# Gating mix with the high and low parts of its weights side by side in one product of 256 columns, and the last B gate placed between its groups

## The reference, cut to what matters

```python
def spatial_gating(u, v, ln_g, ln_b, w_s, b_s):
    v = layer_norm(v, ln_g, ln_b)
    vb = v.reshape(b, nb, SGU_BLOCK, SGU_GROUPS, SGU_GROUP_DIM)      # 4 blocks of 128 tokens, 4 groups of 128
    w = jnp.where(mask[None], w_s, jnp.zeros_like(w_s))              # 4 matrices, 128 x 128
    mixed = jnp.einsum('gts,bnsgc->bntgc', w, vb) + b_s.T[None, None, :, :, None]
    return u * mixed.reshape(b, s, SGU_WIDTH)
...
y_b = (multiscale_pool(b_x, pool_w[i], pool_scale[i]) * jax.nn.silu(b_z)) @ w_b_out[i]
```

## Time and profile before

| what | value |
|---|---|
| median of 3 runs | 1369.49 us (1369.45 to 1371.21) |
| profiled execution | 1370.01 us, span of its trace 1368.2 us |
| PE busy | 1357.1 us, 99% of the span |
| DVE, ACT, POOL busy | 709.3, 561.5, 555.1 us |
| mean granted TensorE clock | 0.999 of full speed |

### The profile page before, as it was taken

How to read it: one execution, slowest core, us unless ns; L and a number is a source line. 1 busy time by engine, 2 the same in 40 slices (tenths; PEclk the granted TensorE clock), 3 DMA queues, 4 the chain that set the end, 5 groups by cost and what they waited for, 6 DMA issues and landing times.

```text
span 1368.2 us, 15972 instructions
## 1 busy us (share of the span) xinstructions
PE 1357.1 (99%) x6426; PEld 1141.0 (83%) x6426; DVE 709.3 (52%) x1063; ACT 561.5 (41%) x871; POOL 555.1 (41%) x233
## 2 busy tenths in 40 slices
PE   9999999999999999999999999999999999999998
PEld 8778888888888888888888888888888888888887
DVE  7986454155553333265768864451555532242743
ACT  6554463355552222224444554542555422222242
POOL 2334242534334444444353442424433444444443
PEclk9999999999999999999999999999999999999999
DMA  7222222322222323322242222222322222323232
GB/s 213 87 68 85 75 93 65 93 80 90 77 78 98 102 92 94 122 93 93 92 116 93 72 90 70 84 62 93 92 78 77 92 93 93 106 94 108 98 100 95
DMA packets 67834, 126.56 MB, mean 92 GB/s; under 512 B 8480, under 2 KB 37424, under 8 KB 67760
## 3 DMA queue, kind: packets, MB, share of 16 engines
q1 hardware_dynamic: 66528, 124.98, 28.8%
q10 hardware_dynamic: 1232, 0.55, 0.1%
HBM read 123.41 MB, written 2.10 MB: 92 GB/s over the span
## 4 chain that ended last, share of the span: by engine, by line
PE 89%; DVE 7%; ACT 2%; DMA 1%; SPq 1%; issue 0%; ACTq 0%; DVEq 0%
PE ps L484 29%; PE ps L486 29%; PE ps L485 29%; DVE n_t L1430 1%; DVE trail_a L1466 1%; DVE h_lo L1305 1%; PE ps L733 1%; PE ps L668 1%; PE ps L769 1%; PE ps L655 1%; ACT w_hi L941 0%; DVE trail_b L1466 0%; DMA pos_i<-pos_in 0%; SPq L396 0%; DVE small L1447 0%
## 5 line engine op out<-in xcount | busy, mean ns | idle before, releaser
L459 POOL TENSOR_TENSOR w_lo<-w_raw,w_hi 128x1024 fp32r<-128x1024 f32 x222 | 546.4, 2465 | 787.8 <-ACT w_hi L941 787.8
L484 PE MATMUL ps<-h_hi,w_hi 128*128 128x512 f32 (+1 forms) x1160 | 453.1, 391 | 1.4 <-DVE h_lo L1305 1.3
L486 PE MATMUL ps<-h_hi,w_lo 128*128 128x512 f32 (+1 forms) x1160 | 450.5, 388 | 0.0
L485 PE MATMUL ps<-h_lo,w_hi 128*128 128x512 f32 (+1 forms) x1160 | 450.3, 388 | 0.0
L941 ACT ACTIVATE w_hi<-w_raw 128x1024 fp32r<-128x1024 f32 x227 | 238.5, 1054 | 169.7 <-PE ps L486 164.9
L484 PEld LDWEIGHTS ps<-h_hi,w_hi 128*128 128x128 f32 x1160 | 218.0, 188 | 47.7 <-DVE h_lo L1305 4.1
L486 PEld LDWEIGHTS ps<-h_hi,w_lo 128*128 128x128 f32 x1160 | 217.9, 188 | 44.7
L485 PEld LDWEIGHTS ps<-h_lo,w_hi 128*128 128x128 f32 x1160 | 218.1, 188 | 43.3
L1750 DVE SCALAR_TENSOR_TENSOR m_part<-th,ps 128x512 f32<-128x512 f32 x48 | 33.0, 688 | 236.9 <-PE ps L486 236.8
L1169 ACT ACTIVATE th<-ps 128x512 f32<-128x512 f32 x48 | 28.7, 597 | 182.0 <-PE ps L486 182.0
L484 PE MATMUL ps<-act_hi,w_hi 128*128 128x512 f32 x192 | 75.3, 392 | 0.0
(11 more groups left out here) (324 smaller groups left out, 1923.0 us busy)
## 6 DMA issues: line engine op xcount, KB each, us to landing
w_raw<-w_in SPq DMA_DIRECT2D x180, 512.0 KB, 3.5
w_raw<-w_in SPq DMA_DIRECT2D x92, 128.0 KB, 2.4
w_raw<-w_in SPq DMA_DIRECT2D x36, 256.0 KB, 2.9
x<-x_in SPq DMA_DIRECT2D x8, 256.0 KB, 3.7
w_raw<-w_in SPq DMA_DIRECT2D x32, 64.0 KB, 2.1
out_x<-x SPq DMA_DIRECT2D x7, 256.0 KB, 4.0
p_raw<-p_in SPq DMA_DIRECT2D x2, 512.0 KB, 4.4
w_raw<-w_in ACTq DMA_DIRECT2D x4, 128.0 KB, 3.0
```

Of the source, the lines that this page charges most:

```text
L459: pool.tensor_tensor(w_lo_t[s][:], w_raw_t[s][:], w_hi_t[s][:].bitcast(F32), ALU.subtract).then_inc(w_lo_made, 1)
L484: pe.matmul(o, a_hi, b_hi, start=first, stop=False, skip_group_check=skip)
L485: pe.matmul(o, a_hi, b_lo, start=False, stop=False, skip_group_check=skip)
L486: return pe.matmul(o, a_lo, b_hi, start=False, stop=last, skip_group_check=skip)
```

## The change

The low part of the mix weights is no longer kept in `w_lo_t`, but in the unused second half of the chunk's `w_hi_t` tile. One matmul with the stationary `vn_hi` then streams 256 columns, the high and the low weights of the group (`w_both[:, g::G, :]`), into 256 columns of PSUM, and a second one adds `vn_lo` by the high weights to the first 128 of them. A layer has 32 mix matmuls in place of 48. The two halves are added when DVE takes the mix out: two ops a group in place of one, with a wait between them. A group now needs two banks: groups 0 and 2 are in banks 0 and 1, groups 1 and 3 in banks 2 and 3.

So the order changes too: PE computes groups 0 and 1, then `bz3`, then groups 2 and 3, which wait for `mix_taken` of groups 0 and 1. `bz3` goes to bank 4 and no longer waits for `off_made`; `gb` and `yb` of the first pair take banks 5 and 4 (before 4 and 5), those of the second 6 and 7 as before. DVE makes `rope_tables` before quarter 2 of branch B, and quarter 3 between the groups. ACT does the tanh of `bz3` before the high part of `gb0`.

```diff
-BZ_BANKS, K_BANK = (7, 4, 6, 5), (6, 4)
+BZ_BANKS, K_BANK = (7, 4, 6, 4), (6, 4)
+GATE_BANK, TURN_BANK = (5, 6), (4, 7)
...
-                    pool.tensor_tensor(w_lo_t[s][:, 0:n, :], w_raw_t[s][:, 0:n, :], w_hi_t[s][:, 0:n, :].bitcast(F32),
+                    pool.tensor_tensor(w_hi_t[s][:, G:2 * G, :], w_raw_t[s][:, 0:G, :], w_hi_t[s][:, 0:G, :].bitcast(F32),
                                        ALU.subtract).then_inc(mix_lo_made, 1)
...
+                def mix(g):
+                    last = None
+                    for t in range(TB):
+                        o, v = (g % 2 * 4 + t) * 2 * P, slice(g * P, (g + 1) * P)
+                        pe.matmul(ps[:, o:o + 2 * P], vn_hi[:, t, v], w_both[:, g::G, :], start=t % 2 == 0, stop=False,
+                                  skip_group_check=True)
+                        last = pe.matmul(ps[:, o:o + P], vn_lo[:, t, v], w_both[:, g, :], start=False, stop=True,
+                                         skip_group_check=True)
+                    last.then_inc(mix_ready if g < G - 1 else done(l, "mix"), 1)
+
+                pe.wait_ge(pooled, after(l * G + 3))
+                pe.wait_ge(v_made, after(l * TB + 3))
+                pe.matmul(bank(5), ones_r[:], w_both[:, 0:G, :], start=True, stop=False)
+                pe.matmul(bank(5), ones_r[:], w_both[:, G:2 * G, :], start=False, stop=True).then_inc(wsum_ready, 1)
                 pe.wait_ge(ln_made, after(l * TB + TB - 1))
-                for g in range(G):
-                    pe.wait_ge(pooled, after(l * G + g))
-                    for t in range(TB):
-                        last = mm3(ps[:, g * 512 + t * P:g * 512 + (t + 1) * P], vn_hi[:, t, g * P:(g + 1) * P],
-                                   vn_lo[:, t, g * P:(g + 1) * P], w_hi[:, g, :], w_lo[:, g, :])
-                    last.then_inc(mix_ready if g < G - 1 else done(l, "mix"), 1)
-                pe.wait_ge(off_made, after(l))
-                project(l, "bz3", 5)
+                mix(0)
+                mix(1)
+                pe.wait_ge(act_b_made, after(l * G + 1))
+                project(l, "bz3", 4)
+                pe.wait_ge(mix_taken, after(l * G))
+                mix(2)
+                pe.wait_ge(mix_taken, after(l * G + 1))
+                mix(3)
...
                     if p == 0:
-                        pe.wait_ge(mix_taken, after(l * G + t))
+                        if t % 2 == 0:
+                            pe.wait_ge(mix_taken, after(l * G + 2 + t // 2))
...
-                act.wait_ge(*end_of(l, "mix"))
+                bz(3, 4)
                 weights_up_to(l, "gb0")
-                bz(3, 5)
                 b_high(3)
...
+                    o = g % 2 * 8 * P
+                    both = ps[:, o:o + 8 * P].rearrange("p (t u s) -> p t u s", t=TB, u=2)
+                    to = mix_t[:, g, :].rearrange("p (t s) -> p t s", t=TB)
+                    settle(dve.scalar_tensor_tensor(to, both[:, :, 1, :], sm("ln_col", g),
+                                                    over(mix_off[:, g, :], [P, TB, P], 1), ALU.mult, ALU.add))
+                    dve.scalar_tensor_tensor(to, both[:, :, 0, :], sm("ln_col", g), to, ALU.mult, ALU.add).then_inc(
+                        mix_taken, 1)
...
+                mix_taken_out(0)
+                mix_taken_out(1)
                 gate_z(3)
                 gate_p(3)
+                mix_taken_out(2)
+                mix_taken_out(3)
                 b_low(3)
```

More of the change, by code:

```diff
@@ L467, in _ @@
                     kept = keep[:].unsqueeze(1).broadcast_to([P, G, P // 2])
-                    part_hi, part_lo = w_hi_t[s][:, 0:G, 0:P // 2], w_lo_t[s][:, 0:G, 0:P // 2]
+                    part_hi, part_lo = w_hi_t[s][:, 0:G, 0:P // 2], w_hi_t[s][:, G:2 * G, 0:P // 2]
                     pool.tensor_tensor(part_hi, part_hi.bitcast(F32), kept, ALU.mult).then_inc(mix_hi_kept, 1)
@@ L609, in front @@
                 project(l, "bz2", 6)
-                w_hi, w_lo = chunk(l, "mix")
-                pe.matmul(bank(5), ones_r[:], w_hi[:, 0:G, :], start=True, stop=False)
-                pe.matmul(bank(5), ones_r[:], w_lo[:, 0:G, :], start=False, stop=True).then_inc(wsum_ready, 1)
-                pe.wait_ge(ln_made, after(l * TB + TB - 1))
-                for g in range(G):
-                    pe.wait_ge(pooled, after(l * G + g))
-                    for t in range(TB):
-                        last = mm3(ps[:, g * 512 + t * P:g * 512 + (t + 1) * P], vn_hi[:, t, g * P:(g + 1) * P],
-                                   vn_lo[:, t, g * P:(g + 1) * P], w_hi[:, g, :], w_lo[:, g, :])
-                    last.then_inc(mix_ready if g < G - 1 else done(l, "mix"), 1)
-                pe.wait_ge(off_made, after(l))
-                project(l, "bz3", 5)
+                w_both, _ = chunk(l, "mix")
+                def mix(g):
[11 more added lines that the diff above has]
+                pe.matmul(bank(5), ones_r[:], w_both[:, G:2 * G, :], start=False, stop=True).then_inc(wsum_ready, 1)
+                pe.wait_ge(ln_made, after(l * TB + TB - 1))
+                mix(0)
[6 more added lines that the diff above has]
+                mix(3)
             def gate_b(l, d, b, before, n):
@@ L687, in pair_c @@
                 k_at = slice(2 * PAIR * QK, 2 * PAIR * QK + PAIR * P)
-                kb, fill = K_BANK[p], 10 - K_BANK[p]
+                kb, gate, turn = K_BANK[p], GATE_BANK[p], TURN_BANK[p]
                 if p == 0:
@@ L710, in pair_c @@
                 if p == 0:
-                    gate_b(l, d, fill, mix_taken, l * G + 3)
-                    branch_b(l, d, fill + 1, act_b_made, l * G + 3)
-                else:
[L714 to L717, removed]
+                    gate_b(l, d, gate, mix_taken, l * G + 3)
+                    branch_b(l, d, turn, act_b_made, l * G + 3)
+                else:
+                    gate_b(l, d, gate, cz_taken, n - 2)
+                    branch_b(l, d, turn, act_c_made, n - 1)
+                gate_b(l, d + 1, gate, gb_tanh, l * KD + d)
+                branch_b(l, d + 1, turn, yb_taken, l * KD + d)
                 pe.wait_ge(k_made, after(lp))
@@ L724, in pair_c @@
                                           lambda t: q_tok[:, t, 1, :])):
-                    if p == 0 and b == 4:
+                    if p == 0 and b == gate:
                         pe.wait_ge(gb_tanh, after(l * KD + d + 1))
-                    if p == 0 and b == 5:
+                    if p == 0 and b == turn:
                         pe.wait_ge(yb_taken, after(l * KD + d + 1))
@@ L1117, in pair_c @@
                 d, head, n, lp = 4 * p, PAIR * p, l * G + PAIR * p, l * 2 + p
-                kq, kb, fill = f"kq{p}", K_BANK[p], 10 - K_BANK[p]
+                kq, kb, fill = f"kq{p}", K_BANK[p], GATE_BANK[p]
                 act.wait_ge(k_ready, after(lp))
@@ L1542, in front @@
                 b_low(1)
+                rope_tables()
                 gate_z(2)
@@ L1554, in front, with mix_taken_out @@
                 dve.wait_ge(off_made, after(l))
-                rope_tables()
-                for g in range(G):
+                def mix_taken_out(g):
                     if g < G - 1:
@@ L1626, in pair_c @@
                 d, head, n, lp = 4 * p, PAIR * p, l * G + PAIR * p, l * 2 + p
-                kb, fill = K_BANK[p], 10 - K_BANK[p]
+                kb, turn = K_BANK[p], TURN_BANK[p]
                 dve.wait_ge(k_squared, after(lp * 2 + 1))
@@ L1661, in pair_c @@
                                   ALU.mult).then_inc(k_made, 1)
-                branch_b(l, d, fill + 1)
-                branch_b(l, d + 1, fill + 1)
+                branch_b(l, d, turn)
+                branch_b(l, d + 1, turn)
                 for b, (o, h, gain) in enumerate((
```

## The result

The changed kernel took 1374.71 us (median of 7 runs) against 1369.45 for the kernel before (7 runs), 5.3 us more: ratio 1.0034, 95% interval 1.0025 to 1.0044. So it is slower, by less than half a per cent. One of the seven runs was a slow one of 2762.84 us at the full granted clock; the ratio leaves it out, and the median of the other six is 1374.67. The ratios given here are not quotients of the medians (1374.71 over 1369.45 is 1.0038); the difference is about 0.5 us. The profiled execution took 1373.87 us (span 1372.1), the second fastest of the seven.

The account below looks back on a forecast made before the run. PE's chain of matmuls was taken to bound the kernel, busy 1357.1 of 1368.2 us. To 1369.5 us came 2.0 for later queries and 1.6 for one clock fall: 1373.1 us, range 1370.7 to 1375.2.

Parts of the forecast that it names:

- The step of the matmuls: In PE's mix: a pair of one 256-column and one 128-column matmul costs 0.230 us, between 0.222 and 0.240.
- The wait for `bz3`'s low part: After mix groups 0 and 1, PE waits 2.0 us a layer for POOL's low part, swallowing the first half's saving.
- `mix_taken` of groups 0 and 1, `rope_tables`, `yb0`: Around the mix: groups taken out before PE wants them, tables in DVE's idle 3.60 us, later `yb0` load; all cost nothing.
- The queries' wait: Before the queries, PE waits 0.6 us for group 2's `mix_taken`; queries start 1.0 us later a layer, 2.0 in all.
- The clock: Behind each new PE wait, about one chance in two of falling to the 1.2 GHz level: once in two layers, 1.6 us.
- rival 2: The clock falls behind the new wait in both layers: +2.0 + 3.2, 1374.7 us; chance 0.25.
- a clock that always falls: Sign behind the new waits: the prediction is wrong if the clock never falls or always does.
- rival 1: The clock stays up behind both new waits: +2.0 us alone, 1371.5 us or 0.15%; chance 0.29.
- rival 3: `bz3`'s low part is ready when PE arrives, no waits: 1367.5 us, or 1366.2 without the queries' wait; faster has chance 0.07.

## Why the prediction was right, and what was off

The forecast was 1373.1 us in a range of 1370.7 to 1375.2; 1374.71 lies in it, 1.6 above the forecast. The waits and their causes were right. The number of falls of the clock was a guess from two rows: the time is covered because the range was made to hold both falls, and that the forecast came so near owes something to luck.

- *The step of the matmuls.* 0.230 a pair was taken, 0.232 measured in the stream. The stride of the 256 columns cost nothing.
- *The wait for `bz3`'s low part.* 2.0 us with a start 3.88 after the mix's; 1.92 of idle time and 3.87 measured, in both layers. It was shown by taking away its cause: with the high part early the stage is 1.9 to 2.1 us shorter.
- *`mix_taken` of groups 0 and 1, `rope_tables`, `yb0`.* All costed at nothing, and in the changed kernel none of them ends a wait of PE.
- *The queries' wait.* 0.6 us and 1.0 in sum a layer were taken, 0.32 and 0.87 + 0.08 measured: the chain from `bz3` to group 2 was shorter by 0.1 us. The idle time reads less than the delay, since it is counted from the modelled end of the last key matmul (115.48 + 0.28 = 115.76), while without a wait the query would have started one step of 0.12 behind that matmul's start, at 115.60: 0.48 of delay.
- *The clock.* This is the term that was mis-sized. One fall was taken, 1.6 us, at one chance in two per wait. The filled waits give its worth: 2.7 us between the changed kernel and the one with eight extra matmuls, by the ratios, so nearer to two falls than to one. The mean clock says the same, about 1.9 falls more than before. The time of 1374.7 is rival 2's. In the profiled execution, of 1373.87 us, the clock fell behind one of the two new waits, as forecast. The prediction named a clock that always falls as a sign of being wrong; over the runs it came near to that, though where it fell in those without a trace is not known.
- *The clock staying up (rival 1).* The clock fell behind 1.92 us, and once behind 1.08. The Trainium skill, "TensorE: Matmul & The Clock Gate", section "HAM oscillation — how this bites in real kernels", speaks of longer waits than these. By that rule alone the clock would have stayed up, and the runs decide against it.
- *Faster without the first wait (rival 3).* Its mechanism did not come by itself, but the kernel with `bz3`'s high part early makes it so. The rival had the queries 11.25 us behind the mix's start then (104.25 to 115.5); 11.25 and 11.07 were measured.

Open is why the totals of the two kernels with `bz3` early but no filling lie 0.7 us or more above what their stages give, and what exactly of PE's work before a short wait decides whether the clock falls.

## What to carry to other kernels

Before work is moved forward on the busiest engine, ask of each thing it needs by how much it is early today: here 1.58 us, and the move was 3.5. A saving on the busiest engine is real only if its suppliers move with it; the cause then is one line on another engine, not the new instructions. And a wait of PE of one or two microseconds can cost its length and a fall of the clock behind it; a few useless matmuls in it are a cheap way to see how much of a loss is the clock.

## What the runs showed of the hardware

- The granted clock fell to the 1.2 GHz level behind waits of 1.92 and once even of 1.08 us, behind matmuls of 128 columns, each fall costing about 1.6 us (9.89 against 8.27 for the same stretch). Behind waits of 5.17 and 4.49 us it cost 1.9 and 2.2 us of busy time. An idle time of 0.86 us behind matmuls of 512 columns cost nothing measurable (1371.97 with four extra matmuls, 1371.99 with eight). Where a fall comes differs from execution to execution.
- A matmul of 256 columns whose columns come from two places 2 KB apart steps as fast as one with contiguous columns: 0.232 us for it and one of 128 together, where the steps of the two kinds apart add up to 0.230 (0.119 and 0.111).
- The same op on DVE takes 0.43 us alone and 2.50 to 2.65 us when a subtraction on POOL has started just before it; started 0.38 us ahead of the subtraction it took 0.42. Where both started at 103.40 (the kernel with only `bz3`'s high part early, layer 0) the op took 0.42 and the subtraction 2.69 in place of 2.4. Moving the subtraction 2 us forward brought that into a place where it had not been, in some layers and executions and not in others.
